# First weight tiles of each norm in a buffer of their own, and weight splits two tiles ahead, in a two-layer streaming encoder

## What is computed

```python
h = _rms(x, p['g_mix_pre'])
proj = h @ p['w_in']
q1, q2, k1, k2, v, ux, ug, ga, gb = jnp.split(proj, idx, axis=-1)
...
branch_a = o.reshape(B, T, ATTN_V) @ p['w_branch_attn']
...
branch_b = (hl * jax.nn.gelu(ug)) @ p['w_branch_lru']
m = jax.nn.sigmoid(ga) * branch_a + jax.nn.sigmoid(gb) * branch_b
x = x + _rms(m @ p['w_out'], p['g_mix_post'])
f = jnp.square(jax.nn.relu(_rms(x, p['g_mlp_pre']) @ p['w_up'])) @ p['w_down']
x = x + _rms(f, p['g_mlp_post'])
```

## Time and profile before

| what | value |
|---|---|
| median of three runs | 2166.58 us |
| the profiled execution | 2163.76 us |
| its span in the profile | 2161.6 us |
| mean granted TensorE clock | 0.991 |
| ACT busy | 956.5 us (44%) |
| DVE busy | 1078.6 us (50%) |
| DMA, mean over the span | 80 GB/s |

### The profile page before, as it was taken

The page is one execution under the profiler, slowest core; times in us unless marked ns, Lnnn a source line. Parts: engine busy times, 40 slices in busy tenths (PEclk is TensorE's granted clock), DMA queues, the critical chain, the costliest instruction groups (busy, mean ns, idle before and its releaser), DMA issues.

```text
span 2161.6 us, 39635 instructions
## 1 busy us (share of the span) xinstructions
PE 2066.7 (96%) x15925; PEld 2013.3 (93%) x15925; DVE 1078.6 (50%) x2102; ACT 956.5 (44%) x1573; POOL 255.8 (12%) x283
## 2 busy tenths in 40 slices
PE   4999999999999899999989999999999989999997
PEld 4899999998999899999979999999999979999997
DVE  3366666665445432243455666666554363223434
ACT  4346464647235441233353656565652353312324
POOL 1303030200020220021012111111001102001200
PEclk9999999999999999999999999999999999999999
DMA  3313131312332223333322222222222323233332
GB/s 98 102 50 102 50 102 50 92 50 69 88 88 69 82 85 88 88 88 88 88 69 83 69 82 66 86 64 78 69 70 87 88 69 88 79 87 88 88 89 70
DMA packets 308155, 172.05 MB, mean 80 GB/s; under 512 B 7296, under 2 KB 303568, under 8 KB 308016
## 3 DMA queue, kind: packets, MB, share of 16 engines
q1 hardware_dynamic: 300720, 155.47, 24.9%
q0 software_dynamic: 7232, 14.49, 2.4%
q10 hardware_dynamic: 64, 0.13, 0.0%
HBM read 158.86 MB, written 11.21 MB: 79 GB/s over the span
## 4 chain that ended last, share of the span: by engine, by line
PE 81%; DVE 8%; ACT 7%; issue 3%; DMA 1%; ACTq 0%; DVEq 0%
PE PJ L529 60%; PE PJ L672 5%; PE PJ L541 4%; PE PX L698 3%; PE PX L736 3%; DVE w_lo L1356 2%; ACT w_hi L920 2%; PE PX L541 1%; DVE s L1558 1%; PE PX L546 1%; PE PX L714 1%; PE PX L624 1%; PE PX L692 1%; DVE uc L1595 1%; ACT L946 0%
## 5 line engine op out<-in xcount | busy, mean ns | idle before, releaser
L1356 DVE TENSOR_TENSOR w_lo<-w_raw,w_hi 128x1024 fp32r<-128x1024 f32 x288 | 385.5, 1351 | 360.7 <-ACT w_hi L920 360.1
L529 PE MATMUL PJ<-h_hi,w_hi 128*128 128x272 f32 x2304 | 491.0, 295 | 17.6 <-DVE w_lo L1356 16.7
L529 PE MATMUL PJ<-h_lo,w_hi 128*128 128x272 f32 x2304 | 475.9, 288 | 0.0
L529 PE MATMUL PJ<-h_hi,w_lo 128*128 128x272 f32 x2304 | 475.3, 288 | 0.0
L920 ACT ACTIVATE w_hi<-w_raw 128x1024 fp32r<-128x1024 f32 x288 | 298.4, 1047 | 209.8 <-DMA w_raw<-in_w_down 115.7
L529 PEld LDWEIGHTS PJ<-h_hi,w_hi 128*128 128x128 f32 x2304 | 362.9, 190 | 22.7 <-issue 12.4
L529 PEld LDWEIGHTS PJ<-h_hi,w_lo 128*128 128x128 f32 x2304 | 362.6, 189 | 0.0
L529 PEld LDWEIGHTS PJ<-h_lo,w_hi 128*128 128x128 f32 x2304 | 361.9, 189 | 0.0
L529 PE MATMUL PJ<-u_hi,w_hi 128*128 128x272 f32 x960 | 198.0, 288 | 3.4 <-DVE w_lo L1356 3.4
L529 PE MATMUL PJ<-u_lo,w_hi 128*128 128x272 f32 x960 | 197.8, 287 | 0.0
L529 PE MATMUL PJ<-u_hi,w_lo 128*128 128x272 f32 x960 | 197.3, 287 | 0.0
(11 more groups left out here) (293 smaller groups left out, 3761.9 us busy)
## 6 DMA issues: line engine op xcount, KB each, us to landing
w_raw<-in_w_in SPq DMA_DIRECT2D x112, 512.0 KB, 3.8
w_raw<-in_w_up SPq DMA_DIRECT2D x64, 512.0 KB, 4.0
w_raw<-in_w_down SPq DMA_DIRECT2D x64, 512.0 KB, 3.6
w_raw<-in_w_branch_attn SPq DMA_DIRECT2D x16, 512.0 KB, 3.6
w_raw<-in_w_branch_lru SPq DMA_DIRECT2D x16, 512.0 KB, 3.6
w_raw<-in_w_out SPq DMA_DIRECT2D x16, 512.0 KB, 3.6
out_prompt_k<-stage POOLq DMA_DIRECT2D x16, 256.0 KB, 2.8
out_prompt_v<-GA POOLq DMA_DIRECT2D x8, 512.0 KB, 3.9
```

The lines of the kernel that those rows point to most:

```text
L529: mm = pe.matmul(PJ[:, buf, half, 0:HT], w[a], src[b][:, k0 + k, HT * half:HT * half + HT], start=first and k == 0 and a + b == 0, stop=en ...
L1356: dve.tensor_tensor(w_lo[:, n.slot, :, :], w_raw[:, n.slot, :, :], w_hi[:, n.hi, :, :].bitcast(F32), ALU.subtract).then_inc(w_lo_ready, 1)
```

## The change

**A buffer of its own.** The first tile behind each norm (pair tile 0, MLP tile 0) is loaded into `first_raw` (its low part `first_lo` in the same place, its high part in w_hi[4], its semaphore w_landed[4]) instead of a slot of the ring; acc_x keeps its place, which the new buffer covers, and the other sums, squares and r2q move behind it. So slot 0 is free for tile 4: SP loads both (`load_apart`, `load_early`) before tiles 1 to 3, behind a wait of its own for the LRU's last step (in the middle of the layer) or for the sum of x's squares (at its end), because the place holds their data until then. Tile 4's load no longer waits for tile 0. At the kernel's start five tiles are loaded instead of four.

**The split of tile 4.** In the MLP ACT splits tile 4 before tile 1's activation, DVE before tile 2's evacuation; among the pair tiles ACT splits it behind tile 1's work and DVE before `qk_tile` of tile 2. Both stood one tile later.

**Two tiles ahead.** From gate 1 to the output tiles, splits take tile n + 2 where they took n + 1; w_hi then has four slots in use instead of two (`deep`), so that `split_hi` doesn't wait for tile_done there.

**The inverse norm.** ACT's logarithm and exponential of r2q move behind `down_four(l, 0, 0)`, which holds the splits of four down tiles.

Three places of the engines' programs follow, before and after, each row an instruction with what it waits for; "xN" are N alike. Lines are those of each kernel, so the same statement has another number after the change.

The diff, cut to its core:

```diff
@@ SBUF places
+        first_raw = at("first_raw", [P, KT, P], F32, R_AT)
+        first_lo = at("first_lo", [P, KT, P], F32R, R_AT)
         acc_x = at("acc_x", [P, NT], F32, R_AT)
-        acc_y = at("acc_y", [P, NT], F32, R_AT + TILE)
+        acc_y = at("acc_y", [P, NT], F32, R_AT + 4576)
...
         def mixer_tile(l, first, r, j):
-            return TileNo(TL * l + first + 4 * r + j, j)
+            return TileNo(TL * l + first + 4 * r + j, j, deep=True, apart=2 * l + 1)
         def pair_tile(l, p, i):
             n = TL * l + 12 * p + i
-            if p == 0 and i < 4:
-                return TileNo(n, i, (0, 1, 2, 4)[i], 0)
+            if p == 0 and i == 0:
+                return TileNo(n, WR, WR, 0, apart=2 * l)
+            if p == 0 and i < 5:
+                return TileNo(n, i % WR, i % WR, 0, apart=2 * l + 1)
...
+        def gate_b_tile(l, i):
+            if i < 2:
+                return TileNo(TL * l + T_GB + i, i, apart=2 * l + 1)
+            return TileNo(TL * l + T_GB + i, i % WR, deep=True, apart=2 * l + 1)
...
@@ SP
+            def load_early(n, source):
+                need(sp, tile_done, n.value - 2 * WR + 1)
+                sp.dma_start(raw(n), source).then_inc(w_landed[n.slot], 16)
+            def load_apart(n, source):
+                sp.dma_start(raw(n), source).then_inc(w_landed[n.slot], 16)
...
+                sp.wait_ge(lru_step, 12 * 8 * (l + 1))
+                load_apart(mlp_tile(l, 0, 0, 0), columns("w_up", l, 0))
+                load_early(mlp_tile(l, 0, 4, 0), columns("w_up", l, 4))
+                for j in range(1, WR):
+                    load(mlp_tile(l, 0, 0, j), columns("w_up", l, j))
+                for j in range(1, WR):
+                    load(mlp_tile(l, 0, 4, j), columns("w_up", l, 4 + j))
...
-            for i in range(WR):
-                sp.dma_start(w_raw[:, i, :, :], pair_source(0, 0, i)).then_inc(w_landed[i], 16)
+            for i in range(WR + 1):
+                load_apart(pair_tile(0, 0, i), pair_source(0, 0, i))
             for l in range(DEPTH):
                 load_layer(l)
                 if l < DEPTH - 1:
-                    for i in range(WR):
+                    sp.wait_ge(x_ssq, 3 * l + 3)
+                    load_apart(pair_tile(l + 1, 0, 0), pair_source(l + 1, 0, 0))
+                    load_early(pair_tile(l + 1, 0, WR), pair_source(l + 1, 0, WR))
+                    for i in range(1, WR):
                         load(pair_tile(l + 1, 0, i), pair_source(l + 1, 0, i))
@@ ACT
             def up_four(l, c, r):
-                    if not (first and j < 3):
+                    if not first:
                         split_hi(n + 1)
+                    elif j == 1:
+                        split_hi(mlp_tile(l, 0, 4, 0))
...
                     for i in range(5):
-                        if p > 0 or i > 2:
+                        if p > 0 or i == 4:
                             split_hi(pair_tile(l, p, i + 1 if i < 4 else 6))
                         if i == 3:
                             split_hi(pair_tile(l, p, 5))
+                        if i == 1 and p == 0:
+                            split_hi(pair_tile(l, p, 4))
...
+                split_hi(gate_b_tile(l, 1))
                 for i in range(8):
-                    n = N + (T_GB + i)
-                    split_hi(n + 1)
+                    n = gate_b_tile(l, i)
+                    if i > 0:
+                        split_hi(gate_b_tile(l, i + 2) if i < 6 else mixer_tile(l, T_WA, 0, i - 6))
...
                     if i == 0:
                         place_o(l, 3, 9)
                         sub_square(l, 3, 0)
+                        split_hi(gate_b_tile(l, 2))
                         load_table(ACT.Exp)
...
                 load_table(ACT.Ln)
                 for i in range(6):
                     if i < 5:
-                        split_hi(out_tile(l, i + 1))
+                        split_hi(out_tile(l, i + 2))
                     mix_out(l, i)
                     if i == 4:
-                        split_hi(out_tile(l, 6))
                         split_hi(out_tile(l, 7))
                         split_hi(mlp_tile(l, 0, 0, 0))
...
                     if c == 0:
+                        down_four(l, c, 0)
                         act.wait_ge(x_ssq, 3 * l + 3)
...
                         act.activation(r2q[:], r2q[:], ACT.Exp, scale=-1.0).then_inc(x_rs, 1)
-                        down_four(l, c, 0)
@@ DVE
             def up_four(l, c, r):
-                    if not (first and j < 3):
+                    if not first:
                         split_lo(n + 1)
+                    elif j == 2:
+                        split_lo(mlp_tile(l, 0, 4, 0))
...
+                        if i == 2 and p == 0:
+                            split_lo(pair_tile(l, p, 4))
                         if p > 0 and i < 4 or i in (2, 3):
                             qk_tile(l, p, i)
                         if i == 2 and p == 0:
-                            split_lo(pair_tile(l, p, 4))
                             split_lo(pair_tile(l, p, 5))
```

More of the change, by code:

```diff
@@ L69, with __init__ @@
 class TileNo:
[L72 to L73 removed]
+    def __init__(self, value, slot, hi=None, held=None, deep=False, apart=0):
+        self.value, self.slot, self.deep, self.apart = value, slot, deep, apart
         self.hi = (slot if deep else slot % 2) if hi is None else hi
@@ L77, in __add__, with landed @@
     def __add__(self, k):
-        return TileNo(self.value + k, (self.slot + k) % WR, deep=self.deep)
+        return TileNo(self.value + k, (self.slot + k) % WR if self.slot < WR else k % WR, deep=self.deep, apart=self.apart)
+    def landed(self):
+        if self.slot == WR:
+            return 16 * (self.apart + 1)
+        return 4 * (self.value - self.slot) + (16 - 16 * self.apart if self.slot == 0 else 16)
 def hybrid_encoder(nc, A, out):
@@ L199, in hybrid_encoder @@
         PX = ctx.enter_context(nc.psum_tensor("PX", [P, 4, 512], F32))
-        w_landed = [sem(f"w_landed{i}") for i in range(WR)]
+        w_landed = [sem(f"w_landed{i}") for i in range(WR + 1)]
         w_hi_ready, w_lo_ready, tile_done, evacuated = map(sem, ("w_hi_ready", "w_lo_ready", "tile_done", "evacuated"))
@@ L249, in out_bank, with raw, low @@
             return PJ[:, 0, half, :]
+        def raw(n):
+            return first_raw[:] if n.slot == WR else w_raw[:, n.slot, :, :]
+        def low(n):
+            return first_lo if n.slot == WR else w_lo[:, n.slot, :, :]
         def mixer_tile(l, first, r, j):
-            return TileNo(TL * l + first + 4 * r + j, j)
+            return TileNo(TL * l + first + 4 * r + j, j, deep=True, apart=2 * l + 1)
         def pair_tile(l, p, i):
             n = TL * l + 12 * p + i
-            if p == 0 and i < 4:
-                return TileNo(n, i, (0, 1, 2, 4)[i], 0)
+            if p == 0 and i == 0:
+                return TileNo(n, WR, WR, 0, apart=2 * l)
+            if p == 0 and i < 5:
+                return TileNo(n, i % WR, i % WR, 0, apart=2 * l + 1)
             hi = 2 if i == 5 else (i + p + (i > 5)) % 2
-            return TileNo(n, i % WR, hi, n - (2 if i in (5, 6, 7) else 1))
+            return TileNo(n, i % WR, hi, n - (2 if i in (5, 6, 7) else 1), apart=2 * l + 1)
+        def gate_b_tile(l, i):
+            if i < 2:
+                return TileNo(TL * l + T_GB + i, i, apart=2 * l + 1)
+            return TileNo(TL * l + T_GB + i, i % WR, deep=True, apart=2 * l + 1)
         def out_tile(l, i):
-            return TileNo(TL * l + T_WO + i, i % WR, deep=i > 5)
+            return TileNo(TL * l + T_WO + i, i % WR, deep=True, apart=2 * l + 1)
         def mlp_tile(l, c, later, j):
-            return TileNo(TL * l + (T_MLP + 32 * c) + later + j, j, deep=True)
+            n = TL * l + (T_MLP + 32 * c) + later + j
+            if isinstance(n, int) and n == TL * l + T_MLP:
+                return TileNo(n, WR, WR, 0, deep=True, apart=2 * l + 1)
+            return TileNo(n, j, deep=True, apart=2 * l + 2)
         def trio_bank(j, h):
@@ L525, in gemm @@
                         pe.wait_ge(waits[0], waits[1] + k)
-                    w = (w_hi[:, n.hi, k, :], w_lo[:, n.slot, k, :])
+                    w = (w_hi[:, n.hi, k, :], low(n)[:, k, :])
                     for a, b in ((0, 0), (0, 1), (1, 0)):
@@ L916, in split_hi @@
             def split_hi(n, first=False):
-                act.wait_ge(w_landed[n.slot], 4 * (n.value - n.slot) + 16)
+                act.wait_ge(w_landed[n.slot], n.landed())
                 need(act, tile_done, n.held, first=first)
-                act.activation(w_hi[:, n.hi, :, :], w_raw[:, n.slot, :, :], ACT.Copy).then_inc(w_hi_ready, 1)
+                act.activation(w_hi[:, n.hi, :, :], raw(n), ACT.Copy).then_inc(w_hi_ready, 1)
             def load_table(func):
@@ L1355, in split_lo @@
                 dve.wait_ge(w_hi_ready, n.value + 1)
```

(2 more changed lines are left out.)

36 lines of the change are left out of this document (18 added, 18 removed).

## The result

The changed kernel takes 2149.43 us (median of four runs, 2149.26 to 2150.18) against 2166.45 for the kernel before in the same comparison (2165.35 to 2169.26): ratio 0.992, 95% interval 0.9903 to 0.9937, so 13.6 to 21.0 us less. In a later comparison it took 2151.33 against 2166.25, ratio 0.9934 (0.992 to 0.9947), 14.9 us less. The profiled execution took 2150.18 (span 2148.4); the forecast for it was 2150.4. The median was forecast at 2153.2.

A forecast was written before the change was run, and what follows sets the result against it. PE, busy 96% of the span, was taken as the bound, with its waits. Terms 7.7 + 4.8 + 0.6 + 0.3 = 13.4 off 2163.76 gave 2150.4 profiled; with 2.8 for the median, 2153.2 us, range 2145 to 2161.

The forecast's parts named there:

- Gates: Gate tiles to first branch tile: three w_lo waits per layer go, partly given back to o_lo; 7.7 us less.
- The part given back to o_lo: Within the first branch tile: PE waits for the last o_lo, giving back 0.4 us and 0.55 in the second layer.
- Output and down tiles: Output tile 1 and second down tile: their w_lo waits go in both layers; 4.8 us less.
- The fifth MLP tile: MLP up tiles 4 and 5: the 5.98 us wait becomes 1.5 then 4.5; 0.6 us less in all.
- The clock behind the moved wait: Behind MLP tile 5's new 4.5 us wait: lower granted clock costs 2.0 us, against 2.4 before.
- The fifth projection tile: Fifth projection tile of each layer: w_lo comes 0.15 us earlier per layer; 0.3 us less in all.
- the MLP wait goes: Rival at MLP tile 5: its w_lo keeps pace, 17.1 us gained instead of 0.6, 2136.7 us; chance 0.07.
- the gates stay: Rival at the gates: evacuations pace them, their term near nothing, 5.7 us left in all, 2160.9 us; chance 0.06.
- the clock stays low for two tiles behind the moved wait: Rival behind MLP tile 4's start: 20 us more at the lower clock in each layer, 2173.2 us; chance 0.03.

The follow-up runs named there:

- norm_later: The kernel before with only the inverse norm moved behind the four down-tile splits: 2162.02 us, ratio 0.9973.
- own_buffer: The changed kernel with the splits one ahead and the inverse norm in its old place: 2167.81 us against 2167.07 for the kernel before.
- squares_later: The changed kernel with x's squares and sums moved to the second group of MLP up tiles, behind each tile's split: 2136.58 us, ratio 0.986 to the kernel before.
- after_again: The changed kernel without a further edit, run again in a later comparison: 2151.33 us against 2166.25 for the kernel before.
- squares_before: The kernel before with only x's squares and their sums moved one group of MLP up tiles later: 2159.01 us against 2168.93.
- squares_pair_lo: Changed kernel with squares later, first-pair tile 5 split before tile 2's qk_hi, DVE's w_lo of tile 4 behind tile 2's evacuation: 2136.84 us, ratio 0.9853.
- two_ahead: The kernel before with only the splits moved two tiles ahead, and the w_hi slots this takes: 2157.61 us against 2167.07.

## Why the prediction was right, and where it was off

**Gates, forecast 7.7, measured 8.3.** All six waits went, and the last eighth of the first branch tile waits for o_lo as worked out (0.21 in each layer). The sum by equal matmuls: from gate 1's first matmul at 488.69 before (489.39 after) to the first one behind the o_lo wait that reads o_lo, at 546.49 before (543.24 after), it is 57.80 before and 53.85 after, 3.95 less; in the second layer 58.19 and 53.85, 4.34. The two rows of the kernel before:

```profile
488.69 0.40 PE L529 MATMUL PJ<-h_hi,w_hi 128*128 128x272 f32 x1 [0.46 <-ACT O L1079]
...
546.49 0.28 PE L529 MATMUL PJ<-o_lo,w_hi 128*128 128x272 f32 x1
```

The part given back to o_lo was mis-sized: I had 0.4 and 0.55, and it was 0.21 both times, with which the term would have been 8.65 - 0.42 = 8.2. (The 0.55 does not follow from the working: in the second layer gate 5 ends 1.08 + 0.16 earlier, which leaves 1.65 - 1.24 = 0.4.) The trace after runs 0.7 late there (489.39 against 488.69); with this added I had the last o_lo ready at 543.1 and wanted at 542.7, and it was ready at 542.83 (the row of DVE below) and wanted at 542.67.

```profile
542.11 0.72 DVE L1919 TENSOR_TENSOR o_lo<-O,o_hi 128x544 fp32r<-128x544 f32 x1 [1.27 <-ACT o_hi L1339]
```

**Output and down tiles, forecast 4.8, measured 5.3.** All four waits are gone: the second down tile follows the first without one, and the inverse norm's table load, now at 803.23, holds nothing up. By equal matmuls the output tile gave 0.6 and 0.7 in the two layers, the down tile 2.0 and 2.0. `norm_later` shows the down tiles' part alone, 5.0 in the medians, 3.6 in the waits.

**The fifth MLP tile, forecast 0.6 and a wait of 1.5 and then 4.5.** PE's waits are 1.45 and 4.36, 1.47 and 4.39; in `own_buffer`, which stands within 0.1 us of the trace before at gate 4 (510.59 against 510.53), tile 4 begins at 717.33, where the prediction put tile 2's evacuation at 717.3. The reason given, that squares and sums stand ahead of tile 5's split, is shown by `squares_later`: without them both waits go. That the largest of the waits gave nothing was the main point of the forecast, and `own_buffer` measures it: 0.7 us more than before, by its interval from 1.3 less to 3.3 more.
The clock behind the moved wait I took at 2.0 in both layers, and the clock before at 2.4 in both. The granted clock over the 7.5 us after tile 5's start, in the first layer of the changed kernel and of `own_buffer` (columns as above):

```profile
723.50:731.00 7.50, 7.50 (x48) 7.50 (x49) 2.19 (x2) 2.26 (x3) 1.35 (x1) 0.77 0.00 0
```

```profile
727.98:735.48 7.50, 7.49 (x40) 7.50 (x41) 2.19 (x2) 2.26 (x3) 1.35 (x1) 0.63 0.00 0
```

After the same wait (4.36 and 4.39) PE stood at the lower level (1.2 GHz) for so much of the stretch that it cost (1 - 0.77) x 7.5 = 1.7 in one execution and (1 - 0.63) x 7.5 = 2.8 in the other; the second layers repeat this (0.79 and 0.61), and so does `after_again` (0.77 in both). The price I took lies between; it is not one number. Nor is that of the 5.98: in the kernel before's second layer, for which I took the first layer's 2.4 too, the stretch behind it has 0.79 and costs 1.6.

```profile
1778.35:1785.85 7.50, 7.50 (x49) 7.50 (x50) 4.67 (x6) 3.36 (x5) 1.36 (x1) 0.79 0.00 1
```

So by equal matmuls the term is a gain of 0.5 in the first layer and a loss of 0.2 in the second.

**The fifth projection tile, forecast a gain of 0.3, measured a loss of 1.0.** The wait fell by 0.18 per layer (forecast 0.15), and DVE did come in after POOL's first qk_lo. The Trainium skill ("SBUF — State Buffer", section "Who interferes with whom") says that the one that starts first holds the port for its whole instruction. The trace agrees (1.55 where 1.22 is the time alone, 3.65 where 2.68 is); who comes next, which the page leaves open, was DVE. The clock is what the term had wrong: its bounds allow that the shorter wait costs less clock, not that it costs more. Here are the second layer's 7 us behind the wait, before and after:

```profile
1132.21:1139.21 7.00, 7.00 (x47) 7.00 (x48) 1.31 (x6) 2.36 (x4) 0.45 (x1) 0.76 0.01 2
```

```profile
1124.00:1131.00 7.00, 6.92 (x36) 6.92 (x37) 1.34 (x6) 1.17 (x3) 0.00 (x0) 0.56 0.01 2
```

They cost 1.7 and 3.1. This is not one execution's scatter alone: the mean was 0.57 to 0.63 there in all five traces of kernels with the buffer and this wait (the changed kernel, `squares_later`, both again, and `own_buffer`), and 0.76 to 0.78 in five of the six without the buffer (0.63 in `squares_before`). That the buffer makes it so is not shown: `squares_pair_lo`, which has the buffer and a wait of 2.55, has 0.76. In the first layer the term is nothing.

**The sum.** 13.4 forecast; 13.6 in the profiled executions. The four terms by equal matmuls, each from one ahead of its waits to one behind them:

| term | forecast | first layer | second layer | together |
|---|---|---|---|---|
| gates | 7.7 | 3.95 | 4.34 | 8.3 |
| output and down tiles | 4.8 | 2.64 | 2.62 | 5.3 |
| fifth MLP tile | 0.6 | 0.52 | -0.17 | 0.35 |
| fifth projection tile | 0.3 | 0 | -1.0 | -1.0 |
| sum | 13.4 | | | 12.9 |

The other 0.7 lies outside these stretches, where PE's pace differs between the two traces (last section). So the terms are off by +0.6, +0.5, -0.25 and -1.3, which in part cancel, and that the sum meets 13.6 to 0.2 is partly luck. The step from the profiled execution to the median was off by more: I added the 2.8 by which the profile of before stood below its median, and the changed kernel's profiled execution stood 0.75 above its own. The median therefore came out 3.8 below the forecast, within its range; the drop in medians was 17.0 in this comparison and 14.9 in the later one.

**The rivals.** That the MLP wait goes, is out for the change as it stands, and true as soon as its cause is moved (`squares_later`). That the gates stay is out. That the clock stays low for two tiles behind the moved wait is out: its worst row costs 2.9 us (0.61 over 7.5, `own_buffer`'s second layer).

## What to carry to other kernels

A wait is named by the operation that ended it; before moving that operation, read the queue of its engine to the next one of its kind. If other work of the same queue lies between the two, an earlier first one only moves the wait by a tile, and it is that other work that has to go: here squares whose sum PE read some 70 us later held up the weights. An enabling change (a buffer, an earlier load) can measure as nothing and be worth 6 us once the true bound is removed, so it is tested together with that.

## What was not expected of the hardware

PE's pace at full granted clock differs between executions and within one. In 200 us in which PE never paused and the granted clock was 1.00, the matmuls of the MLP numbered, in the first and the second layer (columns as in the stretches above), before:

```profile
860.00:1060.00 200.00, 200.00 (x1602) 200.00 (x1601) 71.33 (x74) 58.48 (x74) 21.70 (x16) 1.00 0.31 90
1880.00:2080.00 200.00, 200.00 (x1610) 200.00 (x1609) 66.86 (x68) 55.26 (x68) 21.82 (x16) 1.00 0.31 90
```

and in `two_ahead`, whose profiled execution was the slowest of its six:

```profile
860.00:1060.00 200.00, 200.00 (x1588) 200.00 (x1587) 70.11 (x73) 58.49 (x74) 21.81 (x16) 1.00 0.30 87
1880.00:2080.00 200.00, 200.00 (x1588) 200.00 (x1588) 65.86 (x69) 54.20 (x67) 21.82 (x16) 1.00 0.30 87
```

1588 against 1610 is 1.4%, 2.8 us in 200. The time from tile to tile says the same without counting: it is the same to 0.01 us for every tile of these stretches, 6.00 and 5.97 us before, 6.05 in both layers of `two_ahead`. In the traces here it holds within a stretch of MLP tiles and changes only where PE paused or ran matmuls of another kind in between (such as the sums over x's squares at 791.1 in the changed kernel). This and the lower clock behind waits make single executions of one kernel scatter by several us (2161.98 to 2168.95 for before on the last chip), which is why a term of 4 us is read from equal matmuls in two traces around one wait, and not from two times. What sets the pace no run here shows.
